# Sample attention in a decoder step: key scores cut into pieces around other TensorE work, the row maximum taken in two halves, and the first two key groups copied by ScalarE

## The reference

```python
def mla_attend_sample(q_lat, q_pe, c_kv, k_pe, past_c, past_kpe):
    T = q_lat.shape[1]
    P = past_c.shape[1]
    s_past = (jnp.einsum('bqhc,bkc->bhqk', q_lat, past_c) + jnp.einsum('bqhr,bkr->bhqk', q_pe, past_kpe)).astype(F32) * MLA_SCALE
    s_new = (jnp.einsum('bqhc,bkc->bhqk', q_lat, c_kv) + jnp.einsum('bqhr,bkr->bhqk', q_pe, k_pe)).astype(F32) * MLA_SCALE
    causal = jnp.tril(jnp.ones((T, T), dtype=bool))
    s_new = jnp.where(causal, s_new, -jnp.inf)
    pr = jax.nn.softmax(jnp.concatenate([s_past, s_new], axis=-1), axis=-1).astype(c_kv.dtype)
    return jnp.einsum('bhqk,bkc->bqhc', pr[..., :P], past_c) + jnp.einsum('bhqk,bkc->bqhc', pr[..., P:], c_kv)
```

## Time and profile before

| What | us |
|---|---|
| Time before, median of 3 runs | 2244.31 |
| Lowest and highest of them | 2239.89, 2245.78 |
| The profiled execution, time | 2247.06 |
| Its span in the trace | 2245.4 |
| First key transpose of the stage | at 689.0 |
| First product of `mla_out` | at 884.8 |

### The profile page before, as it was taken

How to read it: one execution, slowest core, us unless ns; L and a number is a source line. 1 busy time by engine, 2 the same in 40 slices (tenths; PEclk the granted TensorE clock), 3 DMA queues, 4 the chain that set the end, 5 groups by cost and what they waited for, 6 DMA issues and landing times. The chain is left out here.

```text
span 2245.4 us, 38479 instructions
## 1 busy us (share of the span) xinstructions
PE 1956.1 (87%) x15916; PEld 1325.2 (59%) x15916; DVE 700.8 (31%) x1311; ACT 519.8 (23%) x866; POOL 138.2 (6%) x178
## 2 busy tenths in 40 slices
PE   6999986796977786798977999999999999999993
PEld 6999975674455544797854555444544544544441
DVE  4447757224233433335534211111111111111112
ACT  4446622221112322225313111110111110111102
POOL 0000001200030220000010000000000000000000
PEclk9999986696978998899989999999999999999997
DMA  7545520113041430943466999999999999999975
GB/s 213 149 131 132 132 51 3 41 31 107 0 117 55 119 94 16 294 112 124 114 222 272 389 424 424 425 426 424 424 414 414 415 421 411 418 414 413 416 311 171
DMA packets 210228, 543.49 MB, mean 242 GB/s; under 512 B 44520, under 2 KB 168010, under 8 KB 183104
## 3 DMA queue, kind: packets, MB, share of 16 engines
q1 hardware_dynamic: 201746, 532.97, 62.5%
q0 software_dynamic: 7936, 8.68, 1.8%
q10 hardware_dynamic: 438, 0.32, 0.1%
HBM read 524.86 MB, written 28.59 MB: 246 GB/s over the span
## 5 line engine op out<-in xcount | busy, mean ns | idle before, releaser
L2743 PE MATMUL p_u<-w_expert,xgT 128*64 128x256 f32 x1984 | 246.1, 405 | 40.1 <-DMA w_expert<-in_w_up_dram 40.0
L2755 PE MATMUL p_y<-w_expert,hidT 128*64 128x512 f32 x1024 | 232.1, 595 | 0.5 <-DVE hidT L2824 0.5
L2743 PEld LDWEIGHTS p_u<-w_expert,xgT 128*64 128x64 f32 x1984 | 149.9, 146 | 130.2 <-DMA w_expert<-in_w_up_dram 51.9
L2743 PE MATMUL p_g<-w_expert,xgT 128*64 128x256 f32 x1984 | 224.7, 379 | 0.9 <-DVE xgT L2812 0.9
L2743 PEld LDWEIGHTS p_g<-w_expert,xgT 128*64 128x64 f32 x1984 | 142.5, 137 | 85.2 <-issue 18.2
L2706 PE MATMUL p_xg<-low,slot_sel 128*64 128x512 f32 x768 | 178.5, 600 | 4.0 <-DVE slot_sel L2796 4.0
L2755 PEld LDWEIGHTS p_y<-w_expert,hidT 128*64 128x64 f32 x1024 | 70.8, 137 | 133.7 <-issue 133.0
L2817 DVE CAST row<-rowf 128x1 int32<-128x1 f32 x32 | 4.9, 154 | 358.0 <-POOLq L2905 358.0
L2867 ACT ACTIVATE act_g<-p_g 128x256 f32<-128x256 f32 x32 | 12.3, 383 | 450.0 <-PE p_u L2743 450.0
L2902 POOL DMA_INDIRECT x_dram<-y_slots,row x32 | 49.9, 1558 | 991.0 <-DVE y_slots L2828 991.0
L2706 PEld LDWEIGHTS p_xg<-low,slot_sel 128*64 128x64 f32 x768 | 52.8, 138 | 83.8 <-issue 74.6
(11 more groups left out here) (572 smaller groups left out, 2716.1 us busy)
## 6 DMA issues: line engine op xcount, KB each, us to landing
w_expert<-in_w_down_dram SPq DMA_DIRECT2D x64, 2048.0 KB, 21.0
w_expert<-in_w_gate_dram SPq DMA_DIRECT2D x62, 2048.0 KB, 23.6
w_expert<-in_w_up_dram SPq DMA_DIRECT2D x62, 2048.0 KB, 25.2
w_in_raw<-in_w_in_dram SPq DMA_DIRECT2D x32, 1024.0 KB, 5.7
lat<-in_cache_kv_latent_dram SPq DMA_DIRECT2D x128, 128.0 KB, 2.1
w_out_raw<-in_w_out_dram SPq DMA_DIRECT2D x16, 1024.0 KB, 6.9
mem_k_s<-in_cache_mem_k_dram SPq DMA_DIRECT2D x8, 512.0 KB, 6.6
mem_v_s<-in_cache_mem_v_dram SPq DMA_DIRECT2D x8, 512.0 KB, 7.3
```

Of the source, the lines that this page charges most:

```text
L2743: mm = pe.matmul(acc[SL * h:SL * h + SL, 0:FF // 2], xgT[:, t, g // 2, :], tile[:, FF // 2 * h:FF // 2 * h + FF // 2], start=(g < 2 and t ...
L2755: mm = pe.matmul(p_y[SL * h:SL * h + SL, 512 * b:512 * b + 512], hidT[:, j, g, :], w[4 + g][:, D * j + 1024 * h + 512 * b:D * j + 1024 * h ...
```

## The change

`past(x, ci)` is now one pair of products (both partition halves) of one column half x and one part ci (2 is the rotary part). On TensorE the pieces of the next sample's scores stand in four places: (0,0) and (0,1) ahead of the turn of the probabilities, as soon as the key groups 0, 1, 4 and 5 are copied, the queries are there and the exponentials are done; (0,2) behind it; (1,0) behind the value products; (1,1) and (1,2) behind the turn of the output rows. A new semaphore `half_scored` tells VectorE that column half 0 is complete. VectorE takes the maximum of that half (`first_half`) after its copy of the turned probabilities, and after `scored` only that of the other half and one more small maximum of the two. The key groups are shared out by a table: VectorE copies 2, 3, 4, 5, 7, 9, 11, ScalarE 0, 1, 6, 8, 10, and of these 0 and 1 before it waits for the bias. VectorE's sums of the exponentials move behind its copy of the probabilities. ScalarE's last wait for `made` goes.

```diff
+        KEEPS = ((2, 3, 4, 5, 7, 9, 11), (0, 1, 6, 8, 10))
+        half_scored = sem("s_half_scored")
...
-                        pe.wait_ge(kept[k % 2], NI // 2 * b + max(0, k // 2 - 1))
+                        if k < 4:
+                            for e in range(2):
+                                pe.wait_ge(kept[e], len(KEEPS[e]) * b)
+                        else:
+                            e, n = keeper(k - 4)
+                            pe.wait_ge(kept[e], len(KEEPS[e]) * b + n)
...
+                def past(x, ci):
+                    for half in range(2):
+                        out, keys = p_s[64 * half:64 * half + 64, 512 * x:512 * x + 512], slice(1024 * half + 512 * x, 1024 * half + 512 * x + 512)
+                        if ci < 2:
+                            ins = pe.matmul(out, qs[:, ci, :, :].rearrange("p h t -> p (h t)"), kT[:, ci, keys], start=(ci == 0), stop=False)
+                        else:
+                            ins = pe.matmul(out, qps[:, :, :].rearrange("p h t -> p (h t)"), kpT[:, keys], start=False, stop=True)
+                    return ins
...
                     pe.wait_ge(exped, b + 1)
-                    if not isinstance(b, int) or b + 1 < NB:
-
+                    if more:
+                        pe.wait_ge(q_ready, b + 2)
+                        for k in (1, 5):
+                            e, n = keeper(k)
+                            pe.wait_ge(kept[e], len(KEEPS[e]) * (b + 1) + n)
+                        pe.nop(nofuse=True)
+                        for ci in range(2):
+                            past(0, ci)
                         for e in range(2):
-                            pe.wait_ge(kept[e], NI // 2 * (b + 2))
+                            pe.wait_ge(kept[e], len(KEEPS[e]) * (b + 2))
                     for j in range(8):
                         pe.transpose(p_pt[:, 128 * j:128 * j + 128], prob[:, 128 * j:128 * j + 128], S.ident)
                     pe.transpose(p_n[0:64, 64:128], p_new[:, :], S.ident[0:64, 0:64]).then_inc(p_turned, 1)
+                    if more:
+                        past(0, 2).then_inc(half_scored, 1)
...
                     if more:
-                        past(b + 1)
+                        past(1, 0)
                     pe.wait_ge(rows, b + 1)
...
                     if more:
+                        past(1, 1)
+                        past(1, 2)
                         new_keys(b + 1)
...
+                def first_half(b):
+                    dve.wait_ge(half_scored, b + 1)
+                    dve.tensor_reduce(stat[:, 10:11], p_s[:, 0:512], AX.X, ALU.max)
...
-                    dve.tensor_reduce(stat[:, 0:1], p_s[:, :], AX.X, ALU.max)
+                    dve.tensor_reduce(stat[:, 11:12], p_s[:, 512:1024], AX.X, ALU.max)
                     step(dve.tensor_tensor(new[:, :], p_n[0:64, 0:64], S.table("own_causal")[0:64, bass.ds(64 * b, 64)], ALU.add))
+                    step(dve.tensor_tensor(stat[:, 0:1], stat[:, 10:11], stat[:, 11:12], ALU.max))
...
+                    dve.wait_ge(p_turned, b + 1)
+                    dve.tensor_copy(probT[:, 0:4, :].rearrange("p j n -> p (j n)"), p_pt[:, 0:512]).then_inc(p_v, 1)
+                    if more:
+                        first_half(b + 1)
...
                 def body(b, par, it):
+                    if not isinstance(b, int) or b + 1 < NB:
+                        keep(act, act.copy, 1, b + 1, slice(0, 2))
                     act.wait_ge(bias, b + 1)
...
                         queries(b + 1)
-                        keep(act, act.copy, 1, b + 1)
+                        keep(act, act.copy, 1, b + 1, slice(2, None))
...
-                    act.wait_ge(made, NBUF + b + 1)
```

More of the change, by code:

```diff
@@ L1729, in mla_sample, with keeper @@
         NI = 12
+        KEEPS = ((2, 3, 4, 5, 7, 9, 11), (0, 1, 6, 8, 10))
+        half_scored = sem("s_half_scored")
+        def keeper(k):
+            e = 0 if k in KEEPS[0] else 1
+            return e, KEEPS[e].index(k) + 1
         def samples(eng, first, body):
@@ L1796, in body @@
                 def body(b, par, it):
+                    more = not isinstance(b, int) or b + 1 < NB
                     pe.wait_ge(exped, b + 1)
-                    if not isinstance(b, int) or b + 1 < NB:
+                    if more:
[6 more added lines that the diff above has]
+                            past(0, ci)
                         for e in range(2):
-                            pe.wait_ge(kept[e], NI // 2 * (b + 2))
+                            pe.wait_ge(kept[e], len(KEEPS[e]) * (b + 2))
                     for j in range(8):
@@ L1811, in body @@
                     pe.matmul(p_o[0:64, 0:KVL], p_newT[:, :], S.c_tok[0:64, 2, :], start=False, stop=True).then_inc(made, 1)
-                    more = not isinstance(b, int) or b + 1 < NB
                     if more:
-                        past(b + 1)
+                        past(1, 0)
                     pe.wait_ge(rows, b + 1)
@@ L1825, in first @@
                     turn(0, 0, 0)
-                    past(0)
+                    for e in range(2):
+                        pe.wait_ge(kept[e], len(KEEPS[e]))
+                    pe.wait_ge(q_ready, 1)
+                    for x in range(2):
+                        for ci in range(3):
+                            ins = past(x, ci)
+                        if x == 0:
+                            ins.then_inc(half_scored, 1)
                     new_keys(0)
@@ L1832, in _, with keep @@
                 samples(pe, first, body)
-            def keep(eng, copy, parity, b):
-                for k in range(parity, NI, 2):
+            def keep(eng, copy, who, b, some):
+                for k in KEEPS[who][some]:
                     eng.wait_ge(turned, NI * b + k + 1)
@@ L1865, in body @@
                     dve.tensor_copy(st(4, 1), st(4)).then_inc(bias, 1)
-                    if not isinstance(b, int) or b + 1 < NB:
-                        keep(dve, dve.tensor_copy, 0, b + 1)
-                    dve.wait_ge(exped, b + 1)
+                    more = not isinstance(b, int) or b + 1 < NB
+                    if more:
+                        keep(dve, dve.tensor_copy, 0, b + 1, slice(0, None))
+                    dve.wait_ge(p_turned, b + 1)
+                    dve.tensor_copy(probT[:, 0:4, :].rearrange("p j n -> p (j n)"), p_pt[:, 0:512]).then_inc(p_v, 1)
+                    if more:
+                        first_half(b + 1)
                     step(dve.tensor_copy(st(7), st(5, 1)))
@@ L1886, in body, with first @@
                     ins.then_inc(stored, 1)
-                    assert done[0] == 12
-                samples(dve, lambda: keep(dve, dve.tensor_copy, 0, 0), body)
+                    assert done[0] == STEPS
+                def first():
+                    keep(dve, dve.tensor_copy, 0, 0, slice(0, None))
+                    first_half(0)
+                samples(dve, first, body)
             @block.scalar
@@ L1898, in first @@
                     queries(0)
-                    keep(act, act.copy, 1, 0)
+                    keep(act, act.copy, 1, 0, slice(0, None))
                 def body(b, par, it):
+                    if not isinstance(b, int) or b + 1 < NB:
+                        keep(act, act.copy, 1, b + 1, slice(0, 2))
                     act.wait_ge(bias, b + 1)
```

6 lines of the change are left out of this document (2 added, 4 removed).

## The result

The changed kernel takes 2204.57 us (median of 4 runs, 2198.58 to 2207.89), the kernel before 2242.31 on the same chip (median of 4, 2239.89 to 2245.78). The ratio is 0.9834 with a 95% interval of 0.9811 to 0.9857: 1.7% faster; the medians differ by 37.7 us. Timed again later, beside the kernel before once more, the ratio was 0.9871 (0.9829 to 0.9912) and the medians differ by 30.0 us; the two intervals overlap. The profiled execution took 2202.21 us.

The account below looks back on a forecast made before the run. TensorE bounds the samples' attention stage wherever it does not wait. Seven rounds of 18.5 us plus 0.6 and 3.5 make 133.6 against 166.1; with 0.3 for the last sample, 33 us off 2244.31 gives 2211 us, range 2203 to 2226.

Parts of the forecast that it names:

- All of it reaches the end: Samples' attention stage: nothing later is fetched ahead, so the whole gain, 33 us, should reach the kernel's end.
- The round: TensorE's round per sample in the attention stage: from 23.73 us to 18.5 us, summed from its pieces.
- The 0.15 us allowed for switches: TensorE's queue, each round: allowance for four more half-array to whole-transpose switches and some waits, between nothing and 0.6 us.
- Group 6 at 3.04 us after the turn's start: Turn of the keys: group 6 waits for VectorE's copy of group 2 and starts 0.40 us late.
- SP once 0.6 us late: Page loads: five sets of 19.0 us land at 111.6 us, sample 7's turn is due at 111.0.
- Two stretches at half clock, 3.5 us: TensorE's clock: two half-rate stretches in seven rounds, 1.8 us lost in each; the ends none and one a round.
- The seven rounds: Attention stage between maxima: 7 x 18.5 + 0.6 + 3.5 = 133.6 us against 166.1, 32.5 us less.
- The split maximum: VectorE's maximum in two halves: chain to the bias 0.34 us shorter, 0.35 us more VectorE work per round off the path.
- the clock in every round: Rival: one half-clock stretch of 1.8 us in every round; gain 24 us, time 2220; chance 0.10.
- costly switches: Rival: TensorE's switches and waits cost 0.15 us each, VectorE's copies come later; gain about 28 us, 2216; chance 0.08.
- moved gaps: Rival: a TensorE piece waits for late queries or exponentials and gaps only move; time near 2240; chance 0.03.
- The loads as a bound: Rival: an SP page set takes 20 us, the last lands 5.6 us late; gain 28 us, 2216; chance 0.06.

Follow-up runs that it names:

- pieces-alone kernel: Changed kernel with the key copies shared as before and the maximum whole, so only the scores in pieces: seven rounds 143.55 us, time 2211.48 us.
- the filled end: Kernel with ScalarE copying three groups first and one rotary page by SP, plus 32 unused transposes in TensorE's wait for the last sample's exponentials: median 2196.13 us.

## Why the prediction was right

Forecast was 2211 us, measured 2204.57, and the direction, the mechanism and most terms hold. The closeness of some sums is luck, as said below.

- **All of it reaches the end**: yes. Behind the stage the changed kernel took 1353.4 us, the one before 1351.0; nothing downstream took the gain back beyond that.
- **The round**: 18.5 expected, 18.59 measured. The turn of the keys with its two pieces was to take 8.03 and took 8.18 (727.60 to 735.78); probabilities with the rotary piece 2.24 and 2.20; values 4.18 and 4.18; the piece behind them 0.93 and 1.01 (742.16 to 743.17); the output turn with its pieces 2.38 and 2.38. A latent piece that stands alone costs 1.01 us, not 0.93, half of a block of two. The 0.15 us allowed for switches has covered most of what the pieces and the turn took more; the pieces-alone kernel, whose sum of 20.50 us has no such allowance, took 20.50.
- **Group 6 at 3.04 us after the turn's start**: at 3.03 (730.63). Counted by starts it is 0.36 us late where 0.40 was expected (729.40 and the 0.87 of two groups); the timeline's 0.19 of idling counts from the modelled end of the group before. The maximum of one half takes the 0.69 that were chosen.
- **SP once 0.6 us late**: mis-sized. A set takes 19.0 us from its release when SP has been idle, and 19.4 back to back. The waits were 0.36 and 1.23 instead of one of 0.6, and they lengthened the rounds by 0.5 us, near the 0.6 of the sum only because the rest hid behind VectorE's copies. So the bound that was called tight binds already: it is why the split maximum brings nothing.
- **Two stretches at half clock, 3.5 us**: one, 1.5 us. The price of one, 1.8, was nearly right, the number was a guess. In the changed rounds every such stretch stands behind a wait for pages; rounds without one have a granted clock of 1.00. Filled gaps leave no half clock, as the page "TensorE: Matmul & The Clock Gate" of the Trainium skill would have it, and the filled end shows it for one gap.
- **The seven rounds**: 133.6 expected, 132.56 measured. Errors work against each other in it. The clock cost 2.0 us less and the waits for pages 0.1 less; the rounds themselves took 1.0 more, as the kernel with one rotary page by SP shows, which has neither wait nor half clock and takes 130.55 us instead of 129.5.
- **The split maximum**: off the path its additional work costs nothing, in the path 0.34 us a round were expected, and it is worth that only without SP's bound. The rule of "VectorE: DVE Perf Modes" in the Trainium skill, to keep operations few, does not decide here: VectorE is busy 9.74 of 18.59 us.
- **What the forecast could not see** is the part ahead of the stage. The forecast took 33 us off the median, the stage gave 34.2 in the traces, and the medians moved by 37.7 and 30.0 us in the two comparisons. What lies between 34.2 and these two does not come from the forecast's terms, and the second comparison would have met 33 us a little more closely from the other side.
- **A slip in the range**: 36.3 us is the gain with the round at 18.5. With 18.4 it is 37.0, which from the lowest time before gives the 2203 that stands there.

Of the rivals, the clock in every round, costly switches and moved gaps did not come. The loads as a bound came in a small way, by 1.6 us of waiting rather than the 5.6 of that case; with the half clock behind the second wait it cost 2.0.

## What to carry to other kernels

When TensorE waits several times in a round for short steps of other engines, work that depends on none of them, cut into pieces as long as each wait, fills the gaps, and the gain is nearly the sum of the waits read from the timeline (4.8 of 5.3 us a round here). Before counting such a gain, compare the new round with the issue time of each transfer queue back to back, since the next bound may stand half a microsecond behind; here the second bound turned two further improvements of a shorter chain into nearly nothing until one line moved two small loads to the other queue. Test each improvement again when the bound has moved: the split maximum was worth 0 to 0.75 us in seven rounds and then 2.2.

## What the runs showed of the hardware

A gap in TensorE's work can cost more than itself. Behind 3.81 us of waiting the next eight transposes took 1.97 instead of 1.09 us and the value products 5.16 or 6.52 instead of 3.67. In the twelve traces without the filling these products took 5.12 to 6.64 us; in the one with 32 transposes for nothing in the gap both were back at full rate. The products of `mla_out` behind them took 10.54 us even so, against 8.85 in the changed kernel, so the filling does not protect what follows the next gaps.

Shorter gaps do it only sometimes. Of the waits for pages of over 1 us in the traces of the changed kernel and its variants, six were followed by half clock (1.17, 1.23, 1.27, 1.41, 1.79 and 3.30 us) and six were not (1.09, 1.18, 1.51, 1.55, 1.58 and 1.59). The length of the gap alone does not decide it.

How long the half clock lasts in unbroken work differs too. Behind the small gaps of the RWKV part TensorE, busy almost without a pause from line 1153 on, was back at full clock after 3 to 5 us in seven traces and after 16 to 18 in six, with the same code. What decides it was not tried. It makes 4 to 10 us of difference at the start of the samples' stage, whose spread over all traces is 14 us.
